# One dense column group fewer for the third token block, value gathers in batches of 32, and another order of SyncE's loads

## The reference, cut to what matters

```
h = h + peer(rmsnorm(h, norm2_g), w_query, key1, key2, expert_u, expert_v)
return rmsnorm(h, norm_f_g)

def peer(...):                        # per token: 8 heads, 16 experts each = 128 slots
    s1, s2 = scores against key1, key2      # 128 keys each
    experts = i1 * 128 + i2  of the 16 best sums;  gates = softmax(best sums)
    u   = expert_u[experts]                 # (128 slots, 2048)
    act = gelu(u . t) * gates
    out = sum over slots of act * expert_v[experts]
```

## Time and profile before

| | |
|---|---|
| median of 3 runs | 4118.6 us (4117.06 to 4122.15) |
| the profiled execution's own time | 4121.56 us |
| its span, first to last instruction | 4119.7 us |
| mean granted TensorE clock | 0.975 |
| PE / VectorE / ScalarE / POOL busy | 93% / 65% / 30% / 32% |
| moved by DMA | 947.49 MB, 230 GB/s over the span |

### The profile page before, as it was taken

How to read it: one execution, slowest core, us unless ns; L and a number is a source line. 1 busy time by engine, 2 the same in 40 slices (tenths; PEclk the granted TensorE clock), 3 DMA queues, 4 the chain that set the end, 5 groups by cost and what they waited for, 6 DMA issues and landing times.

```text
span 4119.7 us, 53033 instructions
## 1 busy us (share of the span) xinstructions
PE 3846.6 (93%) x19109; PEld 3285.3 (80%) x19109; DVE 2685.7 (65%) x3538; ACT 1221.4 (30%) x1299; POOL 1317.4 (32%) x918
## 2 busy tenths in 40 slices
PE   8999999998999999999999999999988888788887
PEld 5888777786887888888888877777778888788886
DVE  7556788478526645456666657777846666677775
ACT  4333323343324222223333331122223332222222
POOL 1100000422111454551000038888522322245533
PEclk9999999999999999999999999999999999899998
DMA  4574554764933645457777778778867878777773
GB/s 175 193 221 146 172 173 157 237 209 151 319 123 138 196 161 186 165 194 230 249 243 243 256 244 285 277 251 274 291 257 300 307 299 303 280 286 289 289 297 133
DMA packets 270602, 947.49 MB, mean 230 GB/s; under 512 B 36178, under 2 KB 81762, under 8 KB 192506
## 3 DMA queue, kind: packets, MB, share of 16 engines
q1 hardware_dynamic: 93264, 445.68, 30.1%
q0 software_dynamic: 71072, 290.70, 19.8%
q10 hardware_dynamic: 106176, 210.00, 16.2%
HBM read 892.05 MB, written 238.31 MB: 274 GB/s over the span
## 4 chain that ended last, share of the span: by engine, by line
PE 41%; DMA 12%; DVE 10%; POOL 7%; issue 6%; ACT 3%; SPq 0%; ACTq 0%; DVEq 0%; POOLq 0%
PE mm L2125 11%; PE mm L2127 10%; PE mm L2126 10%; DMA raw<-stream 10%; DVE acc L2026 4%; POOL gv L701 4%; POOL el L694 3%; ACT whi L780 3%; PE pv L2125 2%; PE pv L2126 2%; PE pv L2127 2%; DVE wlo L1231 1%; DMA gv<-ev_d,idx_v 1%; DVE h L2007 1%; DMA gl<-up_d 1%
## 5 line engine op out<-in xcount | busy, mean ns | idle before, releaser
L1231 DVE TENSOR_TENSOR wlo<-raw,whi 128x2048 fp32r<-128x2048 f32 x329 | 756.7, 2300 | 691.1 <-ACT whi L780 674.0
L780 ACT ACTIVATE whi<-raw 128x2048 fp32r<-128x2048 f32 x378 | 723.8, 1915 | 643.6 <-DMA raw<-stream 322.1
L2125 PE MATMUL mm<-t_hi,whi 128*128 128x512 f32 x2048 | 807.4, 394 | 44.4 <-DVE wlo L1231 39.0
L2126 PE MATMUL mm<-t_lo,whi 128*128 128x512 f32 x2048 | 802.3, 392 | 0.0
L2127 PE MATMUL mm<-t_hi,wlo 128*128 128x512 f32 x2048 | 801.3, 391 | 0.0
L2026 DVE SCALAR_TENSOR_TENSOR acc<-gv,ac,acc 128x2048 f32<-128x2048 f32 x254 | 596.4, 2348 | 116.7 <-DMA gv<-ev_d,idx_v 108.1
L2125 PEld LDWEIGHTS mm<-t_hi,whi 128*128 128x128 f32 x2048 | 387.5, 189 | 138.7 <-ACT sgl L1072 27.1
L2127 PEld LDWEIGHTS mm<-t_hi,wlo 128*128 128x128 f32 x2048 | 387.2, 189 | 82.0
L2126 PEld LDWEIGHTS mm<-t_lo,whi 128*128 128x128 f32 x2048 | 387.7, 189 | 77.5
L694 POOL DMA_INDIRECT el<-up_d,idx_e x128 | 219.0, 1711 | 566.3 <-DMA up_d<-sgl 527.6
L738 POOL DMA_INDIRECT gv<-ev_d,idx_v x128 | 195.6, 1528 | 614.9 <-DVE acc L2026 549.3
(11 more groups left out here) (476 smaller groups left out, 7314.6 us busy)
## 6 DMA issues: line engine op xcount, KB each, us to landing
raw<-stream SPq DMA_DIRECT2D x380, 1024.0 KB, 5.7
ev_d<-stream ACTq DMA_DIRECT2D x128, 1024.0 KB, 6.5
up_d<-sgl ACTq DMA_DIRECT2D x128, 256.0 KB, 2.7
g_d<-gst ACTq DMA_DIRECT2D x12, 2048.0 KB, 11.5
spill<-stage ACTq DMA_DIRECT2D x44, 256.0 KB, 2.0
gl<-up_d SPq DMA_DIRECT2D x80, 128.0 KB, 2.2
gg<-g_d SPq DMA_DIRECT2D x9, 1024.0 KB, 11.0
gg<-g_d SPq DMA_DIRECT2D x6, 1536.0 KB, 17.3
```

The source lines that it names most:

```text
L780: act.activation(whi[:, k, :], raw[:, k, :], ACT.Copy).then_inc(hi_done, 1)
L1231: dve.tensor_tensor(wlo[:, k, :], raw[:, k, :], whi[:, k, :].bitcast(F32), ALU.subtract)\
L2125: pe.matmul(out, lh, rh, start=start, stop=False)
L2126: pe.matmul(out, lh, rl, start=False, stop=False)
```

## The change

`G1` becomes 9: nine narrow down groups and seven wide ones; the third block is gathered for columns 0 to 71 and its value gathers may start when column 71 is stored. `SLOTS2` deals 7 slots to groups 1 to 8, 11 to groups 9 to 14, and 6 to the last one. `BATCH1` becomes 32: four batches, and 64 value gathers ahead of the row gathers. In SyncE's down loop `load_down` of unit u = 8g+v+1 is issued ahead of gg and gl of iteration (g, v), where it was issued after gl; the first three are issued ahead of the loop as before, and the last group's loop begins at its second unit.

```diff
-G1 = 10
+G1 = 9
-BATCH1 = 12
+BATCH1 = 32
-BATCHES1 = _counts(SLOTS, (BATCH1, SLOTS // BATCH1), (SLOTS % BATCH1, 1))
+BATCHES1 = _counts(SLOTS, (BATCH1, SLOTS // BATCH1))
-SLOTS2 = _counts(SLOTS, (7, G1 - 1), (12, G2 - 1), (5, 1))
+SLOTS2 = _counts(SLOTS, (7, G1 - 1), (11, G2 - 1), (6, 1))
...
+            load_down(0, 0)
+            load_up(7)
+            load_down(0, 1)
+            load_down(0, 2)
             for g in range(GROUPS_D - 1):
                 for v in range(8):
-                    if g or v not in (1, 2):
-                        load_down(g, v)
-                    if g == 0 and v == 0:
-                        load_up(7)
-                        load_down(0, 1)
-                        load_down(0, 2)
+                    u = 8 * g + v + 1
+                    if u > 2:
+                        load_down(u // 8, u % 8)
                     if v == 0:
...
                     sp.wait_ge(up_out[v % 2], _up_count(4 * g + v // 2 + 5))
                     nt_ = TD if g + 1 >= G1 else TE
                     sp.dma_start(gl[:, v % 2, 0:nt_], up_d[8 * g + 8 + v, :, 0:nt_]).then_inc(up_in[v % 2], 16)
-            for v in range(8):
+            for v in range(1, 8):
                 load_down(GROUPS_D - 1, v)
```

## The result

Three runs gave 3965.12, 3975.7 and 3982.71 us, median 3975.7 us, against 4118.6 before: ratio 0.9649, 95% interval 0.9613 to 0.9684. I had forecast faster, but 4035 us in 3980 to 4095, so the time lies outside the range by 4 us, on the side of rival 1 (3969 us).

A forecast was written before the change was run, and what follows sets the result against it. The prediction took a ring of waits through raw loads to bound the down stage, and POOL's gathers the plain units. Terms of -66 and -18 us took 4121.6 to 4037.6; less 3.0 for the median, 4035 us, range 3980 to 4095.

The forecast's parts named there:

- rival 1: Down stage: DMA keeps up and PE alone decides; groups of 50 and 70 us, 3969 us; chance of under 4000 us 0.17.
- the plain units: Units from 2466 to 2912 us, before the down stage: BATCH1 32 lets 13.3 go from 12.22 to 10.89 us, saving 17.7.
- The ring as the bound: Down stage: raw load, split, gate, accumulation, act_low, gl issue, next raw; 14.71 us per two narrow units, 19.95 per two wide.
- "I take 9" for raw's landing: Narrow down groups: raw loads assumed to land in 9 us under denser traffic, giving 6.6 us a unit, 54 a group.
- the same formula: Narrow down groups: landing plus 4.25 us, halved, gives the time a unit; with 9 us landing, 6.6 us.
- my lower bound 50: Best case for a narrow down group: 46.1 us of matmuls plus 3.1 of issue wait, weights never late.
- The 3 + 2 + 3 us of allowance in wide groups: Added to PE's 66.6 us: 3 issue waits, 2 lower clock, 3 late weights near the gg load; 75 us a group.
- The transition group: Last narrow down group, 71.6 us before, whose odd units wait for PE's banks: forecast 58 us, bounds 54 to 71.6.
- the rest: End of the down stage after the other groups, 202.4 us before: forecast as 202.4 - 7 + 2.4.
- my 7: End of the down stage: 7 us gained in the last wide group with gates.
- G1 at +21 us: Down stage: G1 from 10 to 9 moves one group from 54 to 75 us, costing 21 us at the new paces.
- The rule on ring order: Down stage loads: DMA engines take a queue's descriptors in order, so each gl now waits for the 1 MB in front.

The follow-up runs named there:

- the pair of runs: Two kernels with the new SyncE order and BATCH1 12, against the kernel before: G1 9 with slots 7/11/6, 3994.1 us; G1 10 with slots 7/12/5, 3978.6 us.

## Why the prediction was wrong: the mechanism stood, two terms were too large

For the profiled execution I had forecast 4037.6 us, 61.9 too many. The down stage was 67.5 us shorter than forecast (995.3 for 1062.8), and the plain units gave 5.8 less (11.9 for 17.7).

- **The ring as the bound: right.** It was read from the chain of waits, and both the order alone and act_low ahead of the slots confirm it. ScalarE's wait for raw fell from 136.8 us in 528 (2990 to 3518 us, before) to 34.2 in 400.
- **"I take 9" for raw's landing: the step that failed.** The median became 6.8 us in narrow groups, not 9, though DMA moved 347 GB/s, and 6.4 at 390 GB/s with gg in parts. The working held gl's share of the landing (2 us, shown with the wait kept) for the load's own, and added 2 us for load on top. Without the wait the landing does grow, from 5.0 to 6.8 us; whether by load or because raw is now issued 2.9 us after a gl (3296.91 and 3299.78) no run separates. With 6.8 the same formula, (6.8 + 4.25)/2 = 5.5 us a unit, lies under PE's 5.76; with the 3 us stall behind gg the group is 49 to 50 us: measured 50.3, my lower bound 50. That is 18.5 us of the error over eight groups (413.5 measured, 432 forecast): 25.8 too many in seven of them, 7.3 too few in the first, at 61.3 us, in which PE waits once for 18.4 us, as it did before, and which I had priced like the others.
- **The 3 + 2 + 3 us of allowance in wide groups: failed too, and more.** Five groups took 340.4 us, not 375: 34.6 us. The issue wait was no cost of its own, and I counted it beside a wait that it is part of. In the timeline of before, the weight load and the matmul of one stall stand 0.01 us apart and name the same idle time, one as "issue", the other as the split of the weights:

```profile
3242.19 0.29 PEld L2125 LDWEIGHTS pv<-act_room,whi 128*128 128x128 f32 x1 [3.39 <-issue]
3242.20 0.58 PE L2125 MATMUL pv<-act_room,whi 128*128 x1 [3.19 <-DVE wlo L1231]
```

From 2990 to 3518 us the first kind is 31.0 us in 10 times, the second at `pv` 28.9 in 9; with the weights in time the first fell to 1.6 us in 400. With the holes the lower clock level went (granted 1.00).
- **The transition group** took 55.3 us for 58, and the rest 186.1 for 197.8. Most of that is the last wide group with gates: its eight low splits span 67.6 us (from 3785.12 us on) for 82.4 before, 7.8 us more of a gain than my 7. The other term there was too small: the sixth slot at the head of the last group raised PE's stall from 9.8 to 15.2 us, not by 2.4. It is 9.9 us with five slots and the new order, and 15.4 with six and the old one.
- **BATCH1: right in kind.** 18 us by the run without it. In the profiled pair it was 11.9 and not 17.7: the late units did drop from 12.22 to 10.9, but the first 23 units took 12.7 each, against 12.5 before and 12.4 in the run with the old order, where the gain was the full 18. This is scatter between executions: with G1 9 and BATCH1 32 the down stage begins in six profiled ones at 2972.4 to 2978.7 us, mean 2975.8, and with BATCH1 12 in four at 2990.6 to 2998.9, mean 2994.5. The difference is 18.7 us, as forecast.
- **G1 at +21 us** in the down stage: 68.1 - 50.3 = 17.8 at the paces measured, 15.5 by the pair of runs.
- **Rival 1 was what happened**, in its group lengths of 50 and 70 us; its reason, PE alone, holds in wide groups only. I gave it 0.17 and yet ended the range at 3980, above the 3969 us that it gives. My evidence against it, that landings lengthen when loads meet, counted load and not order. I also had in hand a stretch of 386 GB/s and set it aside as a burst.
- **The rule on ring order cut both ways.** By the Trainium skill, "DMA: Bandwidth & Descriptors", "Queues, rings and completion order", each DMA engine takes a queue's descriptors in order; I weighed it only as a risk for gl. gl's median landing did grow, from 2.2 to 5.4 us with the order alone, and VectorE waited 12.4 us for it in 400; but the same rule had held raw behind gl before, for 2 us on the ring itself. The trace agrees with it in both directions.
- **The DMA engines' limit.** 390 GB/s over 184 us, with loads that all come from HBM. The Trainium skill gives about 358 GB/s as one core's limit, half of a stack's rate ("DMA: Bandwidth & Descriptors", Specifications); an estimate by it is 50 us for a narrow group's 17.9 MB. It was no limit here, where one core ran: the group took 46.0 us.

## What to carry to other kernels

When the chain of waits goes in a ring through a load, look at what the issuing engine has queued ahead of it: both the wait it sits behind and the small transfer whose descriptors stand in front. Move the load that the ring needs to the front, and cut large transfers in the same queue into parts placed where nothing is due. A load's landing time is not a property of the load; before pricing it under more traffic, ask how much of it was another transfer's.

## What the runs showed of the hardware that I had not expected

- A 128 KB load of 1 KB pieces issued 0.4 us ahead of a 1 MB load on the same queue delayed that one by about 2 us (median landing 6.8 against 5.0 us, old order with G1 9 against raw ahead with the same wait).
- The DMA engines kept 390 GB/s at a share of 0.99 for 184 us without a hole in PE, and a raw load of 1 MB still landed in 6.4 us at the median.
- The "issue" wait of a weight load before a stalled matmul was that stall seen a second time, not a cost beside it (3.39 and 3.19 us at 3242 us).
- The scatter differs between kernels: the highest of three or four runs lies 18 to 24 us above the lowest in the changed kernel, the order alone and BATCH1 48, and 2 to 11 us in the four kernels with gg in parts. But it is 6 and 8 us in the two with gg whole and the wait for act_low kept, so that the parts are the reason is not shown.
